# TensorE's order in attention: short score products first, values and linear attention with two heads alternating

## What is computed

```python
# dilated attention, per head: three patterns (window, dilation), joined by their log sums
scores = einsum('qd,kd->qk', q, k) * 64 ** -0.5      # causal, masked by the pattern
p = softmax(scores); o = p @ v
# sparse attention, per head: three branches with gates
o = g0 * o_cmp + g1 * o_slc + g2 * o_win
#   o_cmp: 31 compressed key blocks; o_slc: chosen key blocks of 64; o_win: a window of 512
# linear attention, per head, in chunks of 64 tokens (dk 32, dv 64)
a = where(causal, q_dec @ k_inv.T, 0)
o = a @ v + q_dec @ s_in                              # s_in: the state before the chunk
```

## Time and profile before

| | us |
|---|---|
| median of 3 runs | 2732.71 |
| lowest and highest run | 2732.2, 2736.57 |
| span of the profiled execution | 2739.3 |
| TensorE busy | 2649.5 (97%) |
| VectorE busy | 1416.7 (52%) |
| ScalarE busy | 1090.3 (40%) |

### The profile page before, as it was taken

One profiled execution on the slowest core, in us unless ns is written; L12 is line 12 of the kernel. 1 busy time (PEld: TensorE's weight loads), 2 busy tenths in 40 slices (PEclk: granted clock), 3 DMA queues, 4 the chain that ended last, 5 costly groups with the idle time before them and its releaser, 6 DMA issues.

```text
span 2739.3 us, 33416 instructions
## 1 busy us (share of the span) xinstructions
PE 2649.5 (97%) x11814; PEld 2024.4 (74%) x11814; DVE 1416.7 (52%) x2298; ACT 1090.3 (40%) x1649; POOL 51.7 (2%) x64
## 2 busy tenths in 40 slices
PE   8989999999999999999999989999989999899997
PEld 6667888867777788886766668888767667688885
DVE  5867776255553777525256554243352564642434
ACT  3435443146773444324344443233152443431322
POOL 0000000000000000000011000000000110000000
PEclk9999999999999999999989899999998889999999
DMA  4112333221112233323201123323321011233322
GB/s 164 59 54 85 100 92 100 92 69 47 54 54 70 84 98 94 99 93 102 65 24 39 33 67 93 99 92 99 101 73 47 24 39 54 63 98 92 100 92 69
DMA packets 57422, 210.38 MB, mean 77 GB/s; under 512 B 6478, under 2 KB 6880, under 8 KB 56960
## 3 DMA queue, kind: packets, MB, share of 16 engines
q1 hardware_dynamic: 56736, 204.51, 24.2%
q0 software_dynamic: 608, 4.81, 0.5%
HBM read 207.20 MB, written 2.10 MB: 76 GB/s over the span
## 4 chain that ended last, share of the span: by engine, by line
PE 91%; DVE 5%; ACT 2%; issue 1%; DVEq 0%; DMA 0%; SPq 0%; ACTq 0%
PE PS L1071 15%; PE PS L1072 15%; PE PS L1073 15%; PE PS L1087 9%; PE PS L1089 9%; PE PS L1088 9%; PE PS L1242 3%; PE PS L1409 1%; PE PS L1108 1%; PE PS L1408 1%; PE PS L1234 1%; DVE RSTD L1640 1%; PE PS L1099 1%; PE PS L1259 1%; DVE CONV L1709 1%; PE PS L1124 1%
## 5 line engine op out<-in xcount | busy, mean ns | idle before, releaser
L1617 DVE TENSOR_TENSOR WL<-RAW,WH 128x1024 fp32r<-128x1024 f32 x376 | 460.5, 1225 | 666.7 <-ACT WH L545 666.0
L545 ACT ACTIVATE WH<-RAW 128x1024 fp32r<-128x1024 f32 x376 | 397.4, 1057 | 836.5 <-PE PS L1089 578.1
L1071 PE MATMUL PS<-HH,WH 128*128 128x512 f32 x1792 | 727.9, 406 | 1.9 <-DVE WL L1617 1.9
L1072 PE MATMUL PS<-HL,WH 128*128 128x512 f32 x1792 | 709.9, 396 | 0.0
L1073 PE MATMUL PS<-HH,WL 128*128 128x512 f32 x1792 | 709.2, 396 | 0.0
L1071 PEld LDWEIGHTS PS<-HH,WH 128*128 128x128 f32 x1792 | 345.7, 193 | 83.3 <-issue 10.0
L1072 PEld LDWEIGHTS PS<-HL,WH 128*128 128x128 f32 x1792 | 345.0, 193 | 73.5 <-issue 4.5
L1073 PEld LDWEIGHTS PS<-HH,WL 128*128 128x128 f32 x1792 | 343.7, 192 | 74.2
L1089 PE MATMUL PS<-MH,WL 128*128 (+1 forms) x864 | 340.4, 394 | 0.0
L1087 PE MATMUL PS<-MH,WH 128*128 (+1 forms) x864 | 340.4, 394 | 0.0
L1088 PE MATMUL PS<-ML,WH 128*128 (+1 forms) x864 | 340.4, 394 | 0.0
(11 more groups left out here) (273 smaller groups left out, 2852.4 us busy)
## 6 DMA issues: line engine op xcount, KB each, us to landing
RAW<-wstream SPq DMA_DIRECT2D x376, 512.0 KB, 3.6
W<-cmp_w POOLq DMA_DIRECT2D x2, 2048.0 KB, 8.9
X<-xt SPq DMA_DIRECT2D x4, 512.0 KB, 6.8
out<-X SPq DMA_DIRECT2D x8, 256.0 KB, 2.1
TAB<-tables SPq DMA_DIRECT2D x1, 1871.5 KB, 13.0
WS<-spatial_w SPq DMA_DIRECT2D x1, 512.0 KB, 8.6
BS<-spatial_b SPq DMA_DIRECT2D x1, 256.0 KB, 9.3
PW<-pool_w POOLq DMA_DIRECT2D x2, 128.0 KB, 2.3
```

The source lines that it names most:

```text
L545: act.activation(WH[:, b, :], RAW[:, b, :], ACT.Copy).then_inc(w_hi, 1)
L1071: pe.matmul(PS[:, bank, :], WH[:, b, w], HH[:, k, :], start=(k == 0), stop=False)
L1072: pe.matmul(PS[:, bank, :], WH[:, b, w], HL[:, k, :], start=False, stop=False)
L1617: dve.tensor_tensor(WL[:, b, :], RAW[:, b, :], WH[:, b, :].bitcast(F32), ALU.subtract).then_inc(w_lo, 1)
```

## The change

In `scores` the loop over row blocks and heads runs twice: first the short 64-row products of all blocks and heads, with the heads alternating, and then all the full ones. The short product now opens the accumulation, except in row block 0, which shares its bank with row block 2, and the full one closes it. The waits for free banks stand before the short products. In `values` the block loop is outside and the heads alternate inside, and both heads' copies are waited for ahead of the first product. `cmp_scores` and `within` get the same exchange of loops. `gla_values` does all products with the values first, heads alternating, and then all products with the states, heads alternating.

```diff
             def scores(short, full, frees):
                 for i in ROW_ORDER:
                     w = (i + 1) * P
                     for e in range(2):
                         bank = 2 + 3 * e + ROW_AT[i] // T
                         if i and bank in frees:
                             pe.wait_ge(*frees[bank])
-                        last = product(head_banks(e)[:, ROW_AT[i]:ROW_AT[i] + w], e, slice(i * P, w), slice(0, w))
+                        short(head_banks(e)[:, ROW_AT[i]:ROW_AT[i] + w], e, slice(i * P, w), slice(0, w), i > 0)
+                for i in ROW_ORDER:
+                    w = (i + 1) * P
+                    for e in range(2):
+                        last = full(head_banks(e)[:, ROW_AT[i]:ROW_AT[i] + w], e, slice(i * P, w), slice(0, w), i != 2)
                         if i != 2:
                             last.then_inc(at_s[e], 1)
...
             def values(u, vt, PT=PT):
-                for e in range(2):
-                    pe.wait_ge(at_ptc, 2 * u + e + 1)
-                    for k in range(TT):
+                pe.wait_ge(at_ptc, 2 * u + 2)
+                for k in range(TT):
+                    for e in range(2):
                         last = pe.matmul(PS[e * HD:(e + 1) * HD, 2, k * P:T], vt[:, k, e * HD:(e + 1) * HD],
...
             def pair_scores(j):
-                def product(out, e, qs, ks):
+                def short(out, e, qs, ks, start):
                     own = slice(e * HD, (e + 1) * HD)
-                    pe.matmul(out, QS[:, e, qs], KS[:, e, ks], start=True, stop=False)
-                    return pe.matmul(out, QS[own, e, qs], KL[own, ks], start=False, stop=True)
+                    pe.matmul(out, QS[own, e, qs], KL[own, ks], start=start, stop=False)
+
+                def full(out, e, qs, ks, stop):
+                    return pe.matmul(out, QS[:, e, qs], KS[:, e, ks], start=False, stop=stop)
...
                 def gla_values(n):
...
-                        for t in range(TT):
+                    for t in range(TT):
+                        for e in range(2):
+                            v = (2 * n + e) * GLA_DV
                             pe.matmul(PS[e * HD:(e + 1) * HD, 7, t * P:(t + 1) * P], GVTOK[:, t, v:v + GLA_DV],
-                                      AT[:, e, t * P:(t + 1) * P], start=True, stop=False)
-                            for c in (2 * t, 2 * t + 1):
-                                if c:
-                                    cols = slice(c * GLA_CHUNK, (c + 1) * GLA_CHUNK)
-                                    last = pe.matmul(PS[e * HD:(e + 1) * HD, 7, cols], ST[rows, a, c, :], ZT[rows, Z_GQ + a, cols],
-                                                     start=False, stop=(c == 2 * t + 1))
+                                      AT[:, e, t * P:(t + 1) * P], start=(t == 0), stop=False)
+                    for c in range(1, GLA_CHUNKS):
+                        cols = slice(c * GLA_CHUNK, (c + 1) * GLA_CHUNK)
+                        for e in range(2):
+                            a, h = divmod(2 * n + e, 3)
+                            rows = slice(h * GLA_DK, (h + 1) * GLA_DK)
+                            last = pe.matmul(PS[e * HD:(e + 1) * HD, 7, cols], ST[rows, a, c, :], ZT[rows, Z_GQ + a, cols],
+                                             start=False, stop=(c == GLA_CHUNKS - 1))
                     last.then_inc(g_o, 1)
```

More of the change, by code:

```diff
@@ L1213, in _, with scores @@
             conv_ffn(0)
-            def scores(product, frees):
+            def scores(short, full, frees):
                 for i in ROW_ORDER:
@@ L1255, in pair_scores @@
             def pair_scores(j):
-                def product(out, e, qs, ks):
+                def short(out, e, qs, ks, start):
                     own = slice(e * HD, (e + 1) * HD)
-                    pe.matmul(out, QS[:, e, qs], KS[:, e, ks], start=True, stop=False)
-                    return pe.matmul(out, QS[own, e, qs], KL[own, ks], start=False, stop=True)
+                    pe.matmul(out, QS[own, e, qs], KL[own, ks], start=start, stop=False)
+                def full(out, e, qs, ks, stop):
+                    return pe.matmul(out, QS[:, e, qs], KS[:, e, ks], start=False, stop=stop)
                 pe.wait_ge(o_low, 2 * j + 2)
-                scores(product, {})
+                scores(short, full, {})
             first_tiles(base, H_FILL["odd"], 1, NBO, "odd")
@@ L1381, in cmp_scores @@
                     pe.wait_ge(r_done, 6 * l + 3 + jj)
-                    for e in range(2):
-                        rows = slice(e * HD, (e + 1) * HD)
-                        for i in range(TT):
+                    for i in range(TT):
+                        for e in range(2):
+                            rows = slice(e * HD, (e + 1) * HD)
                             last = pe.matmul(PS[:, (4, 7)[e], i * N_CMP:(i + 1) * N_CMP],
@@ L1404, in unit_scores, with short, full @@
                     b, jj = divmod(k, NSA_PAIRS)
-                    def product(out, e, qs, ks):
+                    def short(out, e, qs, ks, start):
                         own = slice(e * HD, (e + 1) * HD)
-                        pe.matmul(out, ZS[:, Z_QS[jj][e], qs], ZS[:, Z_KH[b][e], ks], start=True, stop=False)
-                        return pe.matmul(out, ZS[own, Z_QS[jj][e], qs], ZS[own, Z_KL[b], ks], start=False, stop=True)
+                        pe.matmul(out, ZS[own, Z_QS[jj][e], qs], ZS[own, Z_KL[b], ks], start=start, stop=False)
+                    def full(out, e, qs, ks, stop):
+                        return pe.matmul(out, ZS[:, Z_QS[jj][e], qs], ZS[:, Z_KH[b][e], ks], start=False, stop=stop)
                     pe.wait_ge(k_low, 5 * l + (2, 3, 4, 5, 5, 5)[k])
                     pe.wait_ge(k_high, 5 * l + (2, 3, 4, 5, 5, 5)[k])
-                    scores(product, {2: (u_acc, UNITS * l + k)} | frees)
+                    scores(short, full, {2: (u_acc, UNITS * l + k)} | frees)
                 def unit_values(k):
@@ L1459, in within @@
                         pe.wait_ge(g_am, 3 * l + n)
-                    for e in range(2):
-                        a, h = divmod(2 * n + e, 3)
-                        rows = slice(h * GLA_DK, (h + 1) * GLA_DK)
-                        for t in range(TT):
-                            cols = slice(t * P, (t + 1) * P)
+                    for t in range(TT):
+                        cols = slice(t * P, (t + 1) * P)
+                        for e in range(2):
+                            a, h = divmod(2 * n + e, 3)
+                            rows = slice(h * GLA_DK, (h + 1) * GLA_DK)
                             last = pe.matmul(PS[:, 5 + e, cols], ZT[rows, Z_GK + a, cols], ZT[rows, Z_GQ + a, cols],
@@ L1473, in gla_values @@
                         pe.wait_ge(g_ok, 3 * l + n)
[L1474 to L1485 removed]
+                    for t in range(TT):
+                        for e in range(2):
+                            v = (2 * n + e) * GLA_DV
+                            pe.matmul(PS[e * HD:(e + 1) * HD, 7, t * P:(t + 1) * P], GVTOK[:, t, v:v + GLA_DV],
+                                      AT[:, e, t * P:(t + 1) * P], start=(t == 0), stop=False)
+                    for c in range(1, GLA_CHUNKS):
+                        cols = slice(c * GLA_CHUNK, (c + 1) * GLA_CHUNK)
+                        for e in range(2):
+                            a, h = divmod(2 * n + e, 3)
+                            rows = slice(h * GLA_DK, (h + 1) * GLA_DK)
+                            last = pe.matmul(PS[e * HD:(e + 1) * HD, 7, cols], ST[rows, a, c, :], ZT[rows, Z_GQ + a, cols],
+                                             start=False, stop=(c == GLA_CHUNKS - 1))
                     last.then_inc(g_o, 1)
```

5 lines of the change are left out of this document (removed).

## The result

The changed kernel takes **2613.8 us** (median of 4 runs, 2612.8 to 2621.0) against 2732.5 us (median of 4 runs, 2728.7 to 2736.6) for the kernel before on the same chip: a ratio of **0.957, 95% interval 0.955 to 0.959**. The prediction was 2617 us, range 2588 to 2655. (A run's time is 1.7 us more than its span: the profiled run is the one of 2612.8 us.)

What follows compares the result with a forecast made beforehand. TensorE was taken as the bound: busy 97% of the span, 91% of the chain. Dilated attention 37, units 40 and linear attention 38 sum to 115 us off the median 2732.7: 2617 us, range 2588 to 2655.

Steps and rivals of the forecast that it cites:

- Score stage: Scores in dilated attention and the mixing units, 20 stages: 2.3 us instead of 5.5 each, bounds 2.1 to 4.0.
- the price of a change: In score stages, each change between the 128-row and 64-row form of product costs TensorE 0.15 to 0.2 us.
- Softmax chain: Dilated attention, after the first score: first exponent at about 2.1 us, eight back to back to 6.65, scaling done at 9.25.
- rival A: Softmax chains keep today's length, paced by the maxima: gain only 93 to 98 us, 2637 us; chance 0.14.
- The wait of 1.0 us at the transposes: Dilated attention: TensorE reaches the transposes at 8.25 us and waits 1.0 for the softmax's scaled rows at 9.25.
- Dilated attention, 37 us: Gain over eight pairs: 6.3 us in the first cycle, 29.7 in six middle ones, 1.0 in the last.
- Units, 40 us: Gain in twelve mixing units: 39.3 us to the first transpose, 4 values, 2 compressed scores, less 5 for half clock.
- The bank wait that I read off for unit 4: Mixing unit 4: scores wait for a bank until a VectorE addition ends, 1.4 us after today's first score.
- The values: New order of the values: no gain in dilated attention, where TensorE waits for queries; 0.35 us a mixing unit, 4 in all.
- Linear attention, 38 us: Gain in two mixing layers: 23.8 us in gla_values, 8.1 in within, 6 from the clock around them.
- Rival B: The clock stays low in the mixing units, transposes and part of the values at half rate: 2654 us; chance 0.08.
- Rivals C and D: C: heads don't overlap and head changes cost a drain, 2792 us, chance 0.03. D: change does nothing, 2733 us, chance 0.03.

Runs made afterwards that it cites:

- values_only: The kernel before with only the new order of the values products (heads alternating, both copies waited for first): 2741.8 us, 1.002 of the kernel before.
- by_head: The changed kernel with the short 64-row score products issued head by head instead of with the heads alternating: 2618.0 us, 0.957 of the kernel before.
- seven_shorts: by_head with each head's largest 64-row score product cut into four of 128 columns, so seven short products in a row per head: 2626.1 us in one run.
- heads_apart: The changed kernel with each score stage issuing one head's short and then full products before the other head's: 2644.1 us, 0.966 of the kernel before.

## Why the prediction was right, and where its steps were not

**Score stage, 2.3 us for 5.5: right, 2.22.** So was the price of a change, 0.15 to 0.2: it is 0.18. The working put the overlapping pairs at 0.65 us and the eight full products at 1.3, with 0.35 for the change, the entry and the exit; by starts the pairs take 0.83 and the full ones 1.39, with these inside, so the extras were some 0.08 too high in all.

**Softmax chain: right.** First exponential 2.1 us after the first score, eight back to back to 6.59, last scaled row at 9.10, predicted 2.1, 6.65 and 9.25; ScalarE waited 43.9 us for the maxima and not 56.9. In the trace:

```profile
688.20 0.72 ACT L704 ACTIVATE PB<-PB,NEGMAX 128x512 f32<-128x512 f32 x1 [4.01 <-DVE NEGMAX L1863]
...
692.49 0.19 ACT L704 ACTIVATION_READ_ACCUMULATOR PB<-PB,NEGMAX 128x1 f32 x1
...
692.47 1.28 DVE L1876 TENSOR_SCALAR PB<-PB,RCP 128x128 f32<-128x128 f32 x4
...
693.91 1.27 DVE L1876 TENSOR_SCALAR PB<-PB,RCP 128x128 f32<-128x128 f32 x4
```

That decides against rival A: given the products earlier, the exponentials did run without a pause, and the units' first transposes came after 111.2 us in all, where A had 147.

**The wait of 1.0 us at the transposes did not come in dilated attention.** The tile ends at 8.15 us, head 0's rows are scaled at 7.7, and its ten transposes fill the time until head 1's are. It did no harm to the sum, since the cycle was made from the tile's end: 8.25 + 17.1 = 25.4 predicted, 25.30 measured. TensorE's idle time is 1.3 us ahead of the scores and not 0.7, and before the first short product and not the first full one as I wrote, since one wait stands ahead of the whole stage.

**Dilated attention, 37 us: 37.3.** Made of 7.5 in the first cycle (6.3 predicted), 30.2 in the six (29.7), and -0.5 in the last (1.0). The last is a miss of sign: its 18.81 us have a stretch of 10.2 us at half clock, transposes and values in it, where the kernel before had 6.8. That the total is met to 0.3 us is luck, since the misses of its parts cancel.

**Units, 40 us: 48.1; this is the term that was mis-sized.** The last scaled rows were well placed: 64.7 us summed over a layer's six units predicted, 65.5 and 65.4 measured. But I put the first transpose at the last scaled row. It needs only head 0's rows, and starts 111.2 us after the scores in twelve units and not 129.4. The rest, first transpose to last value, is 85.7 and not 74.1, since head 1 has to be waited for inside it. Together 197.0 and not 203.5. (the earlier trace rows ends some 0.07 us late in each unit; by the measure used here it is 77.2 us and not 78.09.) What is left is between the units, where I had put 3 us of loss and 1 to 2 were lost. The bank wait that I read off for unit 4 came, at 1.0 and 1.1 us, behind the first two short products:

```profile
1441.89 0.95 PE L1414 MATMUL PS<-ZS 64*128 64x384 f32 x6 [0.99 <-DVE ZT L2106]
```

Ahead of unit 1 in the second layer there is one of 1.6 us (on L2122, VectorE's reading of the values' bank) that I had not seen. The 1.0 us on L2034 stands ahead of unit 0, and the kernel before has it too.

**The values:** worth nothing in dilated attention, as predicted, and not 4 us in the units but some -1.5 (243.6 us undone, 245.1 with them): the added waits for the second copy, 17.4 us in thirteen calls, take back what the pairing gives. And values_only took 14 us more than the 2728 that I gave it by the same reasoning. What failed there is that a gain which ends in a wait was costed at nothing; the added wait had a price in the clock.

**Linear attention, 38 us: 41.9.** A call of `gla_values` takes 1.98 us (2.2 predicted) and of `within` 1.09 (1.2): 33.9 us of gain for 31.9, and 8 us came back from the clock around them, where I took 6. I had weighed the Trainium skill's TensorEngine Tiling, "Gotcha 1: PSUM Pressure", by which the 28 instructions of two row groups into bank 7 would go one after the other, 0.8 us more in a call. They take 0.96 us from start to start, 0.07 for two, in the timeline above; before, two took 0.25. The whole call is under my sum without the limit. The trace of this case does not show it. (The two heads also write different partitions of the bank, so heads that share them are not tested.)

**Rival B, the clock low in the units:** it is 0.93 and 0.94 over the units of the two layers, 0.87 and 0.85 before. Some transposes and values do run at half rate, at a cost within the 5 us that I had taken: from first transpose to the end of the values unit 0 takes 10.7 us in the first layer and 7.4 in the second, unit 2 9.1 in the second and 7.8 in the first, 4.6 us together. Half clock in the score stages of units 1 and 4 comes on top; I had not costed it apart. Rivals C and D are excluded by the stage of 2.22 us and the result.

**The sum and the median.** 115 us predicted; 127.3 in the profile and 118.7 between the medians. The 3 us by which the prediction missed the median understate its error: against the execution from which it was made the sum was 12 us low, 8 in the units and 4 in linear attention. Some 9 of these don't show between the medians, since that execution was 6.6 us above its median and the profiled one of the changed kernel 2.7 below.

## What to carry to other kernels

Sort a stage's products by form before anything else: here each change between 128-row and 64-row products costs 0.18 us, and fourteen fewer gave four fifths of the stage's gain; strict alternation of the heads isn't needed, since a product of the other half starts up to four instructions early. Then ask for each gain which chain is next: the same order of the values cost 6 us in the kernel before, was worth nothing beside the new scores, and took 10 us off dilated attention once ScalarE's chain to the queries was shorter. A wait is not free even where it only takes the place of saved work: with one ahead of a stage that works with gaps, the granted clock was 0.88 for 0.93 over six cycles, and useless work in its place was faster.

## What was not expected of the hardware

- TensorE starts an instruction beside one of the other half that stands four ahead of it: 6 ns after head 0's fifth of eight (before), 13 ns after the first of four (by_head), 7 ns after the fourth of seven (seven_shorts).
- A run of four short products takes 0.83 us alone (heads_apart) and 0.83 with a partner each (the changed kernel); 0.18 us is lost at each change of form at full clock.
- Four useless products in each of eight calls made the kernel 10 us faster (2741.8 to 2731.5 us), by a clock of 0.96 for 0.88 in the cycles around them.
